# A chunked recurrence: one transposed step moved from ScalarE to VectorE, GpSimd's decays behind its tables, one product moved forward on TensorE

## The reference

```python
def gdn_chunked(q, k, v, beta, g, S0):          # DeltaNet, 4 heads of 128 x 128
    G = jnp.cumsum(g, axis=-1)
    dec = decay_matrix(G)
    A = eye(c) + einsum('bnhid,bnhjd->bnhij', kb, k) * dec * strict
    rhs = concatenate([v * beta, kb * exp(G)], axis=-1)
    sol = triangular_solve(A, rhs, lower=True, unit_diagonal=True)
    U, Wk = sol[..., :dv], sol[..., dv:]
    qk = einsum('bnhid,bnhjd->bnhij', q, k) * dec
    ...
    def step(S, xs):
        w = u - einsum('bhck,bhkv->bhcv', wk, S)
        o = einsum('bhck,bhkv->bhcv', qg_c, S) + einsum('bhij,bhjv->bhiv', qk_c, w)
        S = exp(gl) * S + einsum('bhck,bhcv->bhkv', kd_c, w)

def ssd_chunked(xdt, g, Bh, Ch, h0):            # SSD, 8 heads of 64 x 128
    cb = einsum('bnhis,bnhjs->bnhij', Ch, Bh) * dec
    y_diag = einsum('bnhij,bnhjp->bnhip', cb, xdt)
    dS = einsum('bnhjs,bnhjp->bnhps', Bh * exp(g_last - G), xdt)
    ...
    y = y_diag + einsum('bnhis,bnhps->bnhip', Ch * exp(G), h_starts)
```

## Time and profile before

| | |
|---|---|
| median of 3 runs | 1615.87 us (1614.2 to 1616.59) |
| the profiled execution: time, and span from its first to its last instruction | 1615.8 us, span 1614.1 us |
| busy, share of the span | TensorE 87%, VectorE 59%, ScalarE 39%, GpSimd 19% |
| the chunk loop (from the first `kk` to the last `ds`) | about 575 to 846 us of the span |
| a steady chunk | 26.0 us |

### The profile page before, as it was taken

How to read it: one execution, slowest core, us unless ns; L and a number is a source line. 1 busy time by engine, 2 the same in 40 slices (tenths; PEclk the granted TensorE clock), 3 DMA queues, 4 the chain that set the end, 5 groups by cost and what they waited for, 6 DMA issues and landing times. The chain is left out here.

```text
span 1614.1 us, 22851 instructions
## 1 busy us (share of the span) xinstructions
PE 1401.7 (87%) x8483; PEld 1252.7 (78%) x8483; DVE 959.8 (59%) x1306; ACT 632.9 (39%) x928; POOL 308.8 (19%) x315
## 2 busy tenths in 40 slices
PE   7899999999999569898887945999953999999990
PEld 5899999999999368888887714888842788788870
DVE  4679656322334246777762537445436889999973
ACT  6231121111000345454441013333312788888873
POOL 0011111000000054545510000100001233333320
PEclk9999999999999879999995557999975999999995
DMA  5011122322110334343313055533232599989837
GB/s 197 26 40 45 46 81 90 106 81 81 66 53 28 136 63 97 67 80 83 64 30 134 1 191 163 170 118 100 64 137 102 179 281 274 277 266 275 276 53 263
DMA packets 107767, 197.00 MB, mean 122 GB/s; under 512 B 57852, under 2 KB 78588, under 8 KB 102564
## 3 DMA queue, kind: packets, MB, share of 16 engines
q1 hardware_dynamic: 92116, 138.57, 27.1%
q0 software_dynamic: 15568, 57.37, 12.9%
HBM read 199.99 MB, written 49.41 MB: 155 GB/s over the span
## 5 line engine op out<-in xcount | busy, mean ns | idle before, releaser
L98 PE MATMUL c_ps<-hn_lo,c_whi 128*128 128x368 f32 x936 | 177.8, 332 | 5.6 <-DVEq L182 5.6
L98 PE MATMUL c_ps<-hn_hi,c_wlo 128*128 128x368 f32 x936 | 177.4, 332 | 0.0
L98 PE MATMUL c_ps<-hn_hi,c_whi 128*128 128x368 f32 x936 | 176.6, 331 | 0.0
L98 PEld LDWEIGHTS c_ps<-hn_lo,c_whi 128*128 128x128 f32 x936 | 160.8, 189 | 5.8 <-issue 5.8
L2357 DVE TENSOR_TENSOR e_winlo<-e_win,e_winhi 128x2048 fp32r<-128x2048 f32 x66 | 151.1, 2291 | 20.8 <-ACT e_winhi L2304 19.4
L98 PEld LDWEIGHTS c_ps<-hn_hi,c_wlo 128*128 128x128 f32 x936 | 160.8, 189 | 0.0
L98 PEld LDWEIGHTS c_ps<-hn_hi,c_whi 128*128 128x128 f32 x936 | 159.8, 188 | 0.0
L2304 ACT CAST e_winhi<-e_win 128x2048 fp32r x66 | 122.7, 1913 | 37.5 <-issue 37.5
L82 ACT CAST c_whi<-c_w 128x1024 fp32r<-128x1024 f32 x40 | 42.1, 1052 | 227.4 <-PE c_ps L98 227.4
L2226 POOL DMA_INDIRECT x_rows<-e_ys,idx_out x33 | 81.6, 2472 | 147.1 <-ACT e_ys L2327 147.1
L526 DVE SCALAR_TENSOR_TENSOR c_y<-c_raw,c_taps,c_y 128x1128 f32<-128x1128 f32 x60 | 83.7, 1394 | 6.1 <-DVE c_y L522 0.2
(11 more groups left out here) (471 smaller groups left out, 2837.5 us busy)
## 6 DMA issues: line engine op xcount, KB each, us to landing
e_win<-in_w_gate_up SPq DMA_DIRECT2D x33, 2048.0 KB
e_wdn<-in_w_down SPq DMA_DIRECT2D x33, 1024.0 KB
c_w<-in_w_in SPq DMA_DIRECT2D x40, 512.0 KB, 3.4
rc_eb<-g_rows SPq DMA_DIRECT2D x10, 1040.0 KB, 6.0
o_land<-in_w_out SPq DMA_DIRECT2D x8, 768.0 KB, 5.1
x_rows<-o_land POOLq DMA_DIRECT2D x12, 512.0 KB, 4.0
rc_gb<-g_rows SPq DMA_DIRECT2D x10, 507.0 KB
kv<-in_xT SPq DMA_DIRECT2D x4, 1104.0 KB, 9.5
```

What stands on the lines that cost most here:

```text
L98: mm = pe.matmul(dst, left(x, k), right(z, k), start=(n == 0 and k == 0), stop=(n == 2 and k == ks - 1))
```

## The change

Five edits, all in `recurrence_phase` and its lists of steps.

1. VectorE: `lm` comes directly behind the four `minus` at the chunk's front; then the copies `m2t`, then the additions `r0`. Before, it was `r0`, `m2t`, `lm`. TensorE now waits for `r0` at the product that reads it.
2. GpSimd: `decay` of a chunk stands behind the tables of the next chunk instead of in front of them.
3. ScalarE: the exponent of `eb` is taken in the chunk that uses it, behind the two `m2` copies, instead of at the end of the chunk before.
4. `yt`: ScalarE's two copies go; VectorE copies `yt` from PSUM itself, and each `vv` addition reads `yt` from PSUM too, not the copy.
5. TensorE: `ks` is issued ahead of the two products of `r3` (the last step of the first inverse), and waits for `kg` and ScalarE's `m8` copies.

```diff
-            for c in range(1, NCH):
-                decay(c - 1)
                 gdn_tables(c)
                 ssd_tables(c)
+                decay(c - 1)
             decay(NCH - 1)
...
-            eb_exp(0)
...
                 take("m2_", m2, (Y[0], X[1]), c, 1)
+                eb_exp(c)
                 for g in range(2):
                     take("m4_", m4, Y, c, g)
...
                 for g in range(2):
                     take("y", y, Z, c, g)
-                    take("yt", yt, X, c, g)
...
                     ssd_exp(c + 1)
-                    eb_exp(c + 1)
...
-                for g in range(2):
-                    wait(v, c, f"mt{g}")
-                    tt_(r0[:, pair(g), :], mt[:, pair(g), :], over(ident, HP), ALU.add)
+                minus(lm, dec_off, slice(0, HA))
                 take("m2t", m2t, (Z[0], X[0]), 0)
                 take("m2t", m2t, (Z[0], X[0]), 1)
-                minus(lm, dec_off, slice(0, HA))
+                for g in range(2):
+                    tt_(r0[:, pair(g), :], mt[:, pair(g), :], over(ident, HP), ALU.add)
...
                 for g in range(2):
-                    wait(a, c, f"yt{g}")
-                    tt_(vv[:, pair(g), :], yt[:, pair(g), :], over(ident, HP), ALU.add)
+                    take("yt", yt, X, g)
+                    tt_(vv[:, pair(g), :], sq_(bank[X[g]]), over(ident, HP), ALU.add)
...
                     prod(Z[g], m2, m2t, g)
+                    wait(v, c, f"r0_{g}")
                     prod(X[g], m2, r0, g)
...
-                for g in range(2):
-                    wait(a, c, f"m8_{g}")
+                wait(v, c, "kg")
+                wait(a, c, "m8_1")
+                products(wide(K, HA), kg, S, all_heads).then_inc(p.sem, 1)
+                for g in range(2):
                     wait(v, c, f"r2_{g}")
                     prod(X[g], m8, r2, g)
-                wait(v, c, "kg")
-                products(wide(K, HA), kg, S, all_heads).then_inc(p.sem, 1)
...
                 for g in range(2):
-                    wait(a, c, f"yt{g}")
+                    wait(a, c, f"y{g}")
+                    wait(v, c, f"yt{g}")
```

More of the change, by code:

```diff
@@ L660 @@
 REC_PE = ["kk", "k", "qk", "m2_0", "m2t0", "m2_1", "m2t1", "xt", "m4_0", "m4t0", "r1_0", "m4_1", "m4t1", "r1_1", "btcb",
-          "m8_0", "r2_0", "m8_1", "r2_1", "r3_0", "r3_1", "ks", "y0", "yt0", "y1", "yt1", "sy", "sds",
+          "m8_0", "r2_0", "m8_1", "r2_1", "ks", "r3_0", "r3_1", "y0", "yt0", "y1", "yt1", "sy", "sds",
           "y2_0", "y2t0", "y2_1", "y2t1", "ds_rhs", "y4_0", "z1_0", "y4_1", "z1_1", "z2_0", "z2_1",
           "w0", "w1", "v", "o0", "ds0", "o1", "ds1"]
-REC_DVE = ["m16_0", "mt0", "m16_1", "mt1", "r0_0", "r0_1", "m2t0", "m2t1", "lm", "qkt", "m4t0", "r1_0", "m4t1", "r1_1",
-           "kg", "xdt", "xdd", "r2_0", "r2_1", "r3_0", "r3_1", "cbt", "cs", "rhs", "vv0", "vv1", "qg", "sy", "z1_0", "z1_1", "ss", "z2_0", "z2_1", "w0", "w1", "s0", "s1"]
-REC_ACT = ["vb", "kd", "m2_0", "m2_1", "m4_0", "m4_1", "bt", "m8_0", "m8_1", "y0", "yt0", "y1", "yt1", "t_exp", "d_exp",
-           "y2_0", "y2t0", "y2_1", "y2t1", "rhs", "y4_0", "y4_1", "s_exp", "eb", "eb_g", "o0", "o1"]
+REC_DVE = ["m16_0", "mt0", "m16_1", "mt1", "lm", "m2t0", "m2t1", "r0_0", "r0_1", "qkt", "m4t0", "r1_0", "m4t1", "r1_1",
+           "kg", "xdt", "xdd", "r2_0", "r2_1", "r3_0", "r3_1", "cbt", "cs", "rhs", "yt0", "vv0", "yt1", "vv1", "qg", "sy", "z1_0", "z1_1", "ss", "z2_0", "z2_1", "w0", "w1", "s0", "s1"]
+REC_ACT = ["vb", "kd", "m2_0", "m2_1", "eb", "eb_g", "m4_0", "m4_1", "bt", "m8_0", "m8_1", "y0", "y1", "t_exp", "d_exp",
+           "y2_0", "y2t0", "y2_1", "y2t1", "rhs", "y4_0", "y4_1", "s_exp", "o0", "o1"]
 REC_POOL = ["q", "t", "qm", "tm", "d", "doff", "d16", "s", "sm"]
@@ L690, in recurrence_phase @@
         p, v = Steps(m, "rc_pe", REC_PE, ["v"]), Steps(m, "rc_dve", REC_DVE)
-        a = Steps(m, "rc_act", REC_ACT, ["s_exp", "t_exp", "d_exp", "eb", "eb_g"])
+        a = Steps(m, "rc_act", REC_ACT, ["s_exp", "t_exp", "d_exp"])
         q = Steps(m, "rc_pool", REC_POOL, ["s", "sm", "q", "t", "qm", "tm", "d", "doff", "d16"])
@@ L706, in recurrence_phase @@
         sq, pick, eps = sb("sq", [P, 2, T]), sb("pick", [P, NQK, 36]), sb("eps", [64, 1])
-        spare = sb("spare", [64, 5])
+        spare = sb("spare", [64, 3])
         lnk, lnq = sq[:, 0], sq[:, 1]
@@ L952, in _ @@
                     ssd_exp(c + 1)
-                    eb_exp(c + 1)
                 else:
                     copy(spare[:, 2:3], eps[:])
-                    copy(spare[:, 3:4], eps[:])
-                    copy(spare[:, 4:5], eps[:])
                 for g in range(2):
```

## The result

| | before | after |
|---|---|---|
| median of 4 runs each | 1615.03 us (1613.0 to 1616.59) | **1629.51 us** (1628.26 to 1633.04) |
| ratio | | 1.0090, 95% interval 1.0073 to 1.0107 |
| the profiled execution: time, span | 1615.8, 1614.1 us | 1633.04, 1631.4 us |
| chunk 0 | 37.58 us | 34.45 us |
| chunks 1 to 8 | 26.00 to 26.02 us each | 27.86, 27.77, 30.83, 29.15, 27.87, 27.83, 27.73, 30.80 us |

The kernel became **slower**, by 0.9%. The forecast was 1611.4 us, faster, in a range of 1604.5 to 1615.0; the result lies outside it. Chunk 0 and chunk 9 won, chunk 0 more than forecast. The steady chunks lost 229.84 - 208.05 = 21.8 us together, and they are no longer equal to each other. The profiled execution is the longest of the four, 3.5 us over their median.

What follows compares the result with a forecast made beforehand. TensorE, busy 23.36 of 26.00 us, was taken to set a steady chunk's pace; 8 x 0.34 = 2.7 us, plus 1.3 (chunk 0) and 0.4 (chunk 9), together 4.4 off 1615.8, gave 1611.4 us, range 1604.5 to 1615.0.

Steps and rivals of the forecast that it cites:

- `lm` in front, and GpSimd's chain 0.06 us later: Chunk front: x transposes lose their 0.97 us wait, products start 0.93 us earlier, but GpSimd's tables start 0.06 us later.
- `ks` in front delays `cs`: TensorE before `r3`: `ks` lasts 0.88 us in a 0.50 us hole, so VectorE reaches `cs` near 702.45, not 701.94.
- All three lie under L830: Chunk 4: `cs` arrivals 701.94 (`ks` free), 702.45 (expected) and 702.87 (`ks` eats all) all fall under GpSimd's L830.
- The pair ends at 703.90: VectorE, chunk 4: `cs` stands until 702.82, then takes 1.08 us, ending at 703.90 against 703.95; front's gain shrinks to 0.05.
- Some 1.3 us: TensorE ahead of `sy`: estimated idle time in a steady chunk while it waits for `cs`.
- The stall moves from `vv` to `qg`: VectorE, chunk 4: L838 starts 0.15 us before `qg` and holds it to 707.82; x update and `ds_rhs` 0.34 us earlier.
- rival 1: `qg` gets in ahead of L838, so `ds_rhs` waits for TensorE only and 0.91 us go whole; 1605.8 us, chance 0.12.
- The cover of `eb` and of the decays: Later decays, `eb` load (1.6 us later) and its exponent still finish before they are needed, costing nothing.
- Chunk 0 and chunk 9: First and last chunks: gains of 1.3 us (0.5 to 1.6) and 0.4 us (0 to 0.5).
- Rival 3: GpSimd keeps access from L838 through both queued decays, so `qg` ends 2.0 us later; 1629.4 us, slower, chance 0.10.
- the 0.14 us of overlap at the end: VectorE against GpSimd tables: a held instruction starts 0.14 us before its holder's recorded end, as read from `kg`.

Runs made afterwards that it cites:

- e_lm_only: The kernel before with only `lm` moved in front and `r0` behind the `m2t` copies; 1596.53 us, ratio 0.9884.
- e_no_ks: The changed kernel with `ks` put back behind `r3` on TensorE; 1594.66 us, ratio 0.9874.
- e_fill: The changed kernel with three extra, unread rounds of key products on TensorE ahead of its wait for `cs` in chunks 1 to 8; 1613.99 us, ratio 0.9993.
- e_cs_one: The changed kernel with the two halves of `cs` made one instruction of 832 elements; 1602.74 us, ratio 0.9926.
- e_no_lm: The changed kernel with `lm` put back behind `r0` and the `m2t` copies; 1610.05 us, ratio 0.9960.
- e_best: The changed kernel with GpSimd's tables reordered, `r0` ahead of `lm`, `cbt` ahead of `r3`, and `qg` behind the x update; 1645.12 us, ratio 1.0181.

## Why the prediction was wrong

By its own steps:

1. **`lm` in front, and GpSimd's chain 0.06 us later: right.** L830 ends 12.32 us into the chunk (12.26 forecast), and TensorE's wait for `lm` is gone.
2. **`ks` in front delays `cs`: right in size.** `cs` is issued at 11.79 (11.75 forecast). With `ks` behind `r3` it is 11.25, where the prediction had 11.24.
3. **"All three lie under L830": wrong for the earliest and the latest.** At 11.25 (the 701.94 of the prediction) `cs` is level with L830's start and goes first (e_lm_only, e_no_ks). The latest, 702.87, lies 0.05 us behind the 702.82 at which the prediction itself lets L830 go. The forecast thus took the gain of edit 1 as lost in any case. By itself it was worth 8 x 1.8 us, and edit 5 undid it.
4. **The pair ends at 703.90: the step that failed.** The prediction let `cs` wait for L830 and then run as one block of 1.08 us. Its own rule, that a waiting VectorE instruction gets in ahead of the next GpSimd one, was applied to the first half and not carried on to the second, which comes up while L836 is queued. The pattern stood in the rows: the first `vv` is held by L836, then L838 runs, and the second `vv` waits for that the earlier trace rows. The price: `cs` ends 14.64 into the chunk instead of 13.20, and `sy` starts at 14.70. By e_fill a steady chunk is then 26.25 instead of the forecast 25.66, 8 x 0.59 = 4.7 us. The split alone is worth more, 26.25 - 24.80 = 1.45 us a chunk by e_cs_one, in which `cs` does end at 13.20; step 6 hides the rest.
5. **TensorE's idle time priced at nothing: the larger miss.** "Some 1.3 us" was 2.42 us. In after the granted clock fell behind it in all eight chunks: 229.84 - 8 x 26.25 = 19.8 us. The prediction had no term for the clock at all, though it read the granted clock of a steady chunk and the section on the time before names chunk 0 as one that starts at the lower level.
6. **The stall moves from `vv` to `qg`, since L838 starts 0.15 us before it: wrong as a rule.** Chunk 0 of after, where nothing holds `cs`, has `qg` issued 0.13 us behind L838's recorded start, and it takes 0.58; so it does in e_no_lm, e_lm_only and five chunks of e_cs_one at 0.08 to 0.14. That is rival 1. In e_lm_only it is the L838 record that grows, to 2.47. What the step was worth shows in e_cs_one: with `cs` ending where step 4 has it, `ds_rhs` doesn't wait and the chunk takes 24.80, 0.86 under the forecast 25.66. In after, too, `ds_rhs` never waits for the x update, where the prediction had it wait some 0.6. Steps 4 and 6 erred in opposite directions; that they partly cancel is luck.
7. **The cover of `eb` and of the decays: right.** ScalarE never waits for `eb` in the steady chunks; the first decay comes at 16.4 of the chunk.
8. **Chunk 0 and chunk 9.** Chunk 9 was right (0.35 us, 0.4 forecast). Chunk 0 won 3.13 instead of 1.3: `sy` starts 1.98 us earlier in the chunk, and 1.15 more comes behind it, 0.90 of that from the wait of `ds_rhs`, which is gone (step 6). Of the 1.98 us, 1.28 is the x transposes' earlier start; the rest was not forecast: the products reach the higher clock at 591.3 of the span instead of 594.2, earlier in the chunk's work, and the chunk's granted clock is 0.85 instead of 0.82. Over the kernels of this study it is 0.82, 0.85 or 0.90 in chunk 0; what sets the moment of the rise is not shown, so this part may be luck.

The difference between forecast and the profiled execution is then 4.7 (steps 4 and 6) + 19.8 (clock) - 1.8 (chunk 0) = 22.7, and 1.1 us less outside the chunk loop, together 21.6. Measured: 1633.04 - 1611.4 = 21.6.

Rival 3 gave 1629.4, which is the measured time, but by another mechanism: its number is a chance hit. It has a decay that keeps `qg` waiting; that does happen, in chunks 3, 4 and 7 of after and on `cs` in e_best, but by one decay, not two, and in after off the path. No rival had the split of `cs` or the clock. The chance given to slower, 0.11, was too small because the only slow case was tied to one queue.

The Trainium skill, "SBUF — State Buffer", section "Who interferes with whom", says that issue order decides which of the two blocks. The runs agree that one excludes the other, and the 0.14 us of overlap at the end stayed: a held `cs` ends 0.44 to 0.45 us behind its holder in after, as `kg` did. Which of two **waiting** instructions is next is what the prediction hung on; there the runs show that after a hold it was mostly the other engine's turn.

## What to carry to other kernels

When a VectorE instruction that reads two SBUF operands comes in pieces, follow **each piece** against the other engine's queue: a pair that is not held keeps its turn (1.08 us), a pair whose first piece is held lets the next GpSimd instruction in between if one is queued (2.17 to 4.91 us). Price an idle TensorE not only at its length but also by what the clock does behind it; here 2.42 us of waiting cost another 1.5 to 4.6 us, and filling the hole with useless products paid. A start that is level with another engine's, give or take half a microsecond, is no place to move work to: 0.54 us decided here between 1594.7 and 1629.5 us.
